# Two transformer blocks on one core: order of the fetches, of the modulation's dots and of the rotary angles at the beginning

## What is computed

```python
mod = jax.nn.silu(c) @ w_ada[l] + b_ada[l]            # w_ada: 1024 x 3072
shift, scale, gate = jnp.split(mod, 3, axis=-1)
h = rmsnorm(x, g_pre[l]) * (1.0 + scale[:, None, :]) + shift[:, None, :]
proj = h @ w_in[l]
...
ang = pos.astype(jnp.float32)[..., None] * inv        # rotary, two bases
cos = jnp.cos(ang); sin = jnp.sin(ang)
...
x = x + gate[:, None, :] * rmsnorm(mixed @ w_out[l], g_post[l])
```

## Time and profile before

| | |
|---|---|
| median of three runs | 1502.81 us |
| lowest, highest | 1500.81, 1503.0 us |
| span of the profiled execution | 1500.5 us |
| what lies around the span, against the median | 2.3 us |
| TensorE busy | 1452.3 us, 97% |
| VectorE, ScalarE, GpSimd busy | 828.7, 683.7, 201.9 us |
| mean granted clock of TensorE | 0.992 |
| chain that ended last | TensorE 84%, VectorE 9%, ScalarE 3% |

### The profile page before, as it was taken

The page is one execution under the profiler, slowest core; times in us unless marked ns, Lnnn a source line. Parts: engine busy times, 40 slices in busy tenths (PEclk is TensorE's granted clock), DMA queues, the critical chain, the costliest instruction groups (busy, mean ns, idle before and its releaser), DMA issues.

```text
span 1500.5 us, 22048 instructions
## 1 busy us (share of the span) xinstructions
PE 1452.3 (97%) x8524; PEld 1226.9 (82%) x8524; DVE 828.7 (55%) x1455; ACT 683.7 (46%) x1302; POOL 201.9 (13%) x319
## 2 busy tenths in 40 slices
PE   7999999899999999999999999989999999999997
PEld 4887876678988888888998777769988888888996
DVE  6678646776645444432275577574754444422474
ACT  4565536676542222221363556676532232321563
POOL 0000000443310000000130222451300000000221
PEclk9999999999999999999999999999999999999999
DMA  9542440004033333333404211503133333332321
GB/s 365 197 167 85 124 157 10 1 2 169 2 99 98 98 98 98 94 95 94 152 3 167 71 57 43 169 16 99 33 109 98 94 92 96 103 105 92 120 85 56
DMA packets 42148, 146.71 MB, mean 98 GB/s; under 512 B 4673, under 2 KB 7121, under 8 KB 41682
## 3 DMA queue, kind: packets, MB, share of 16 engines
q1 hardware_dynamic: 37986, 128.99, 27.2%
q0 software_dynamic: 3072, 15.71, 2.8%
q10 hardware_dynamic: 1008, 0.89, 0.2%
HBM read 141.39 MB, written 4.19 MB: 97 GB/s over the span
## 4 chain that ended last, share of the span: by engine, by line
PE 84%; DVE 9%; ACT 3%; issue 2%; DMA 1%; POOL 0%; DVEq 0%; SPq 0%; ACTq 0%; POOLq 0%
PE B L285 22%; PE B L287 22%; PE B L286 22%; PE CROW_P L285 3%; PE CROW_P L287 3%; PE CROW_P L286 3%; PE B L1789 2%; PE B L2025 1%; DVE AL L1381 1%; DVE WADA L1143 1%; PE CROW_P L1868 1%; ACT T L622 1%; PE CROW_P L1768 1%; ACT AH L622 1%; DVE WL L1110 1%
## 5 line engine op out<-in xcount | busy, mean ns | idle before, releaser
L285 PE MATMUL B<-UH,WH 128*128 128x512 f32 (+1 forms) x1008 | 374.7, 372 | 4.6 <-DVE WL L1110 3.7
L287 PE MATMUL B<-UH,WL 128*128 128x512 f32 (+1 forms) x1008 | 372.3, 369 | 0.0
L286 PE MATMUL B<-UL,WH 128*128 128x512 f32 (+1 forms) x1008 | 372.3, 369 | 0.0
L622 ACT ACTIVATE WH<-RAW 128x1024 fp32r<-128x1024 f32 x174 | 182.6, 1052 | 120.0 <-DMA RAW<-in_stream 111.6
L285 PEld LDWEIGHTS B<-UH,WH 128*128 128x128 f32 x1008 | 190.4, 189 | 38.0 <-issue 5.0
L286 PEld LDWEIGHTS B<-UL,WH 128*128 128x128 f32 x1008 | 190.3, 189 | 32.0
L287 PEld LDWEIGHTS B<-UH,WL 128*128 128x128 f32 x1008 | 190.2, 189 | 32.0
L1110 DVE TENSOR_TENSOR WL<-RAW,WH 128x1024 fp32r<-128x1024 f32 x94 | 116.0, 1240 | 143.8 <-ACT WH L622 143.7
L1462 DVE TENSOR_TENSOR WL<-RAW,WH 128x1024 fp32r<-128x1024 f32 x80 | 98.0, 1226 | 76.7 <-ACT WH L622 73.9
L622 ACT ACTIVATE T<-B 128x256 f32<-128x256 f32 (+5 forms) x186 | 86.5, 465 | 109.9 <-PE B L287 63.3
L622 ACT ACTIVATE T<-T 128x512 f32<-128x512 f32 (+3 forms) x131 | 68.7, 525 | 130.8 <-DVE T L1466 119.2
(11 more groups left out here) (419 smaller groups left out, 3146.2 us busy)
## 6 DMA issues: line engine op xcount, KB each, us to landing
RAW<-in_stream SPq DMA_DIRECT2D x202, 512.0 KB, 3.7
WADA<-in_w_ada SPq DMA_DIRECT2D x8, 1024.0 KB, 16.7
RAW<-in_stream SPq DMA_DIRECT2D x16, 384.0 KB, 3.5
WADA<-in_w_ada SPq DMA_DIRECT2D x2, 2048.0 KB, 11.5
W<-in_w POOLq DMA_DIRECT2D x2, 2048.0 KB, 12.1
X<-in_x SPq DMA_DIRECT2D x2, 1024.0 KB, 11.0
DECAY<-in_decay POOLq DMA_DIRECT2D x1, 2048.0 KB, 9.6
X<-in_x POOLq DMA_DIRECT2D x2, 1024.0 KB, 8.2
```

The costliest lines, as they stand in the source:

```text
L285: nc.tensor.matmul(out, lh, rh, start=start, stop=False, **kw)
L286: nc.tensor.matmul(out, lh, rl, start=False, stop=False, **kw)
L287: return nc.tensor.matmul(out, ll, rh, start=False, stop=stop, **kw)
L622: return nc.scalar.activation(out, in_, func, **kw)
```

## The change

- SyncE's queue fetches x right after c, and pair 0 behind it.
- TensorE warms up with 8 matmuls before the silu row and with 16 behind it, instead of 24 before it.
- SQ has eight tiles, so squares no longer wait for the statistics.
- VectorE does modulation(0) and modulation(1) (`AHEAD = 2`) one after the other; the angles have left its stream.
- GpSimd computes both angles, one after the other, as soon as the positions are there. It has no fused multiply-add here, so each of the three reduction steps is a multiply into T[11] and an add.
- WADA shrinks to 16 rows. The gate's tiles go into rows 8 to 15, once the dots that read these are done, and are fetched ahead of weight tiles 6 and 8.
- The gate's dots run at chunks 6 and 7 (two each) and 8 to 11 (one each). The sines of the second base move from d = 14 to d = 6, `finish_tables(1)` from d = 15 to d = 7.
- DECAY's fetch waits for all 24 dots instead of the scaling of x.

```diff
-        WADA = hb("WADA", 0, [P, ADA, DM])
+        WADA = hb("WADA", 0, [P, 2 * KT, DM])
-        SQ = at("SQ", OFF_U + 16 * KB, [P, 4, SEQ])
+        SQ = at("SQ", OFF_U + 16 * KB, [P, KT, SEQ])
...
             def load_gates(n):
                 m, many = ADA_GATES[n]
-                sp.dma_start(WADA[:, m:m + many, :],
+                sp.wait_ge(E["ada_dot"].sem, 2 * KT - 8 * (1 - n))
+                sp.dma_start(WADA[:, KT + m - 2 * KT:KT + m - 2 * KT + many, :],
...
             sp.dma_start(CROW[0:1, :], a["c"]).then_inc(c_here, 16)
-            load_pair(0)
             for k in range(2):
                 sp.dma_start(X[:, 4 * k:4 * k + 4, :],
...
+            load_pair(0)
...
-                if d in (10, 11):
-                    load_gates(d - 10)
+                if d in (6, 8):
+                    load_gates((d - 6) // 2)
...
-            wait(pool, E["u_t"], KT)
+            def reduced(r, q):
+
+                chain.done(nc.gpsimd.tensor_scalar(q, r, 1.0 / TWO_PI, ROUND, ALU.mult, ALU.add))
+                chain.done(nc.gpsimd.tensor_scalar(q, q, ROUND, None, ALU.subtract))
+                for part in TWO_PI_PARTS:
+                    chain.done(nc.gpsimd.tensor_scalar(T[11][:, :], q, -part, None, ALU.mult))
+                    chain.done(nc.gpsimd.tensor_tensor(r, r, T[11][:, :], ALU.add))
+                E["angle"].mark(nc.gpsimd.tensor_scalar(r, r, PI, -PI, ALU.min, ALU.max))
+
+            pool.wait_ge(pos_here, 16 * 2)
+            chain.done(nc.gpsimd.tensor_copy(T[10][:, :], POSI[:, :]))
+            for n, (r, q) in enumerate(((T[8], T[7]), (T[3], T[2]))):
+                chain.done(nc.gpsimd.tensor_scalar(r[:, :], T[10][:, :], COLS[:, n:n + 1], None, ALU.mult))
+                reduced(r[:, :], q[:, :])
+            wait(pool, E["ada_dot"], ADA)
             fetch(DECAY[:, :, :], a["decay"], decay_here)
...
-                wait(act, E["x_stats"], k - 1 if k >= 4 else 0)
-                return E["x_sq"].mark(f(SQ[:, k % 4, :], src, ACT.Square))
+                return E["x_sq"].mark(f(SQ[:, k, :], src, ACT.Square))
...
-                if d == 14:
+                if d == 6:
                     wait(act, E["angle"], 2)
...
-            modulation(0)
-            dve.wait_ge(pos_here, 16 * 2)
-            chain.done(v.tensor_copy(T[10][:, :], POSI[:, :]))
-            chain.done(ts(T[8][:, :], T[10][:, :], COLS[:, 0:1], None, ALU.mult))
-            chain.done(ts(T[3][:, :], T[10][:, :], COLS[:, 1:2], None, ALU.mult))
-            reduced(T[8][:, :], T[7][:, :])
-            modulation(1)
+            for k in range(AHEAD):
+                modulation(k)
             wait(dve, E["x_rstd"], 2)
...
-                if d == 13:
-                    reduced(T[3][:, :], T[2][:, :])
-                if 12 <= d < 16:
-                    gate_modulation(2 * d - 8, 2 * d - 6)
-                if d == 15:
+                if d in (6, 7):
+                    gate_modulation(2 * d + 4, 2 * d + 6)
+                if 8 <= d < 12:
+                    gate_modulation(d + 12, d + 13)
+                if d == 7:
                     finish_tables(1)
...
             wait(pe, E["converted"], 1)
-            keep_clock(24, UH[:, KT - 1, :], B[4])
+            keep_clock(8, UH[:, KT - 1, :], B[4])
...
+            keep_clock(16, UH[:, KT - 1, :], B[4])
             for k in range(KT):
                 stats(k, B[5])
```

More of the change, by code:

```diff
@@ L59 @@
 FIRST = 6
+AHEAD = 2
 FIRST_STEPS = ([(0, 0), (1, 0), (0, 1), (1, 1)] + [(k, 2) for k in range(2)] + [(2, d) for d in range(3)]
@@ L472, in _ @@
         def _(pool):
+            chain = Chain(pool, "pool_chain")
             def fetch(dst, src, s):
@@ L1131, in _ @@
             E["converted"].mark(v.memset(UH[:, KT - 1, :].bitcast(F32), 0.0))
[L1133 to L1139, removed]
             def dots(m):
-                E["ada_dot"].mark(stt(WADA[:, m, :], WADA[:, m, :], 1.0, (CROW_P if m < 2 * KT else CROW)[:, :], ALU.mult, ALU.mult,
+                row = m if m < 2 * KT else m - KT
+                E["ada_dot"].mark(stt(WADA[:, row, :], WADA[:, row, :], 1.0, (CROW_P if m < 2 * KT else CROW)[:, :], ALU.mult, ALU.mult,
                                       accum_out=DOTS[:, m:m + 1]))
@@ L1191, in _ @@
             for k in range(2, KT):
-                modulation(k)
+                if k >= AHEAD:
+                    modulation(k)
                 u_scaled(k)
@@ L1638, in stats @@
                 wait(pe, E["x_sq"], k + 1)
-                E["x_stats"].mark(mat(bank[:, :], ONES, SQ[:, k % 4, :], start=(k == 0), stop=(k == KT - 1)))
+                E["x_stats"].mark(mat(bank[:, :], ONES, SQ[:, k, :], start=(k == 0), stop=(k == KT - 1)))
             def y_stats(t):
```

## The result

The changed kernel takes 1506.42 us (median of 12 runs, 1504.02 to 1506.8), the kernel before 1502.85 (12 runs beside it, 1500.81 to 1507.24). The ratio is 1.0019, with an interval of 1.0012 to 1.0027: slower by 2.9 us by the ratio and by 3.6 by the medians, small, though the whole interval lies above 1. Another set of 10 runs, later, gave 1504.44 and 1.0015 (1.0004 to 1.0026). The forecast was 1502.9; the medians lie 3.5 us (0.23%) and 1.5 us (0.10%) above it. The profiled execution after has a span of 1504.8 us, where that of before has 1500.5: 4.3 more.

What follows compares the result with a forecast made beforehand. TensorE, busy 97% of the span, was taken as the bound, so only its gaps could close. 1502.8 + 3.0 (later dense run) - 2.9 (gate dots) = 1502.9 us, range 1498.0 to 1506.8.

Steps and rivals of the forecast that it cites:

- The norm comes earlier: Beginning: x lands at 11.4 us, norm's factor comes at 19.2 to 19.5 instead of 22.42, VectorE ready at 19.8.
- Rival 4: Silu row: clock falls, statistics run at half speed, factor at 22; about +0.7, 1503.6 us; chance 0.5 including the main case.
- forecast if the clock were down, 21 to 22: Norm at the beginning: with TensorE's clock down, the factor would arrive at 21 to 22 us.
- What arrives if GpSimd cost nothing: Start of TensorE's dense run: the earlier norm, limited by u_high(1) and the fifth weight tile's landing, gains 1.6 us.
- What the angles cost on GpSimd: Beginning: GpSimd instructions hold VectorE's two-SBUF-input ones, 0.61 us on average, +4.6; dense run 3.0 us later net.
- GpSimd's own time: Beginning: 21 angle instructions from 10.5 us, one-input records 0.77 long, 23 us with waits, done at about 33.
- GpSimd at work beyond 37: Sign at the beginning: GpSimd's angle work lasting past 37 us would point to holds for whole records.
- rival 2: Beginning: GpSimd holds VectorE for whole records, 0.92 on average; 6.8 us plus 1.7 of low clock; 1506.8 us; chance 0.21.
- Gate dots at chunks 6 to 11: Middle: gate loads hidden, the 4.3 us gap near 130 goes, a 1.4 us wait appears; minus 2.9 us net.
- The wait at chunk 12: Chunk 12's first matmul waits for the bank freed by the fourth rotation's multiply: plus 1.4 us.
- Rival 3: Chunk 12: the wait lets the clock fall, as the longer one at 130 did; 1504.3 us; chance 0.1.
- The sum: Whole kernel: 1502.8 + 3.0 - 2.9 = 1502.9 us; what the middle gains is spent at the beginning.

Runs made afterwards that it cites:

- experiment 1: Changed kernel with GpSimd's angle work left out, the angle tiles set to zero: 1500.32 us, 0.998 of the kernel before.
- experiment 3: Changed kernel with all 24 warm-up matmuls ahead of the silu row again: 1503.54 us, 1.0004 of the kernel before.
- experiment 8: Changed kernel run again unaltered, on another occasion; its profiled execution is the "second profile": 1504.44 us, 1.0015 of the kernel before.
- experiment 5: Changed kernel with finish_tables(1) at d = 12 instead of d = 7: 1503.41 us, 1.0002 of the kernel before.
- experiment 2: Changed kernel with a second operation (add 0.0) given to GpSimd's ten one-operation tensor_scalars: 1504.77 us, 1.0008 of the kernel before.
- experiment 7: Changed kernel with GpSimd's angle work replaced by memsets, which only write: one time, 1497.87 us.
- experiment 4: Kernel before with only the gate's part of the change, angles and tables left on VectorE: 1498.97 us, 0.9971 of the kernel before.
- experiment 6: Changed kernel with 24 warm-ups first, all angles on VectorE, second-base sines at d = 13, second tables at d = 14: 1497.78 us, 0.9965 of before.

## Why the prediction came out as it did

**The norm comes earlier: right in some executions, wrong in others.** I had x at 11.4, full clock, the factor at 19.2 to 19.5, and VectorE ready at 19.8. The second half of x is squared from 11.55. Where the clock was up ahead of the row (experiments 1, 3 and 8) x is scaled at 19.5 to 20.1. But in the profile after and in experiment 5 the row took 3.78, some of the 16 warm-ups were slow too (6.3 and 5.7 for all, not 3.95), and the statistics began at 15.2 to 15.4. In experiments 2 and 7 the row was fast (1.98), but then the clock fell while the warm-ups ran (granted 0.50 over 9 to 11 us): they took 5.5, and the statistics began at 12.8 to 13.0. In the six profiles with 8 warm-ups ahead of the row x is thus scaled twice near 19.8, twice near 21.3, twice near 23.7. With 24 ahead of it, as before and in experiments 3, 4 and 6, the row took 1.98 each time. (The statistics behind it took 7.13 in experiments 3 and 6, and 8.83 before and in experiment 4, where TensorE stood idle for 0.8 to 1.0 us ahead of them.) Rival 4 had this clock in mind and put too little on it: it let the statistics run at half speed and added 0.7 us. In fact they run at full speed, but late, and the dense run moves by 3.1. The "forecast if the clock were down, 21 to 22" for the factor was 23.5.

**What arrives if GpSimd cost nothing: right.** Forecast 40.9 to 41.1; experiments 1 and 7 have 41.37 and 41.45. That the factor's first microsecond doesn't arrive is right too: 41.37 comes from x scaled at 20.07, 41.45 from 21.18. The wait for u_high(1) is 0.76 and not 1.2.

**What the angles cost on GpSimd: right mechanism, too large.** Forecast 4.6 net; with the early factor 44.73 - 41.37 = **3.4**. The hold of one instruction was near: forecast 0.48 for one input and 0.95 for two. At 35.74 u_low is stretched by 0.35 beside a one-input instruction, at 41.35 by 1.0 beside a two-input one. What failed is how often the two meet. Ahead of the scaling, four small steps were to cost 1.1, and in the second profile none of them is longer than its plain 0.16. (They can be held: one takes 1.16 in experiment 5, at 17.06, where VectorE had time to spare.) Of the next six instructions each was to wait, for 3.7 in all; they wait 2.8 (in the first profile 1.6, since GpSimd's instruction at 25.21 came second and waited itself while the low half went free). Behind them, where I had 1.0, it is 2.2, because GpSimd worked on until 43. Forecast gross 5.8, found 5.0. The 1.6 between 5.0 and 3.4 are the 1.0 of waits that only experiment 1 has, and the 0.6 by which it scales x later (20.07 against 19.48).

**GpSimd's own time: wrong.** I took 0.77 us for a one-input record from the earlier trace rows, and had the work end at 33; it ended at 43.6. The row I used is a tensor_scalar with two operations, and ten of the 21 have one, which takes 1.50. So the instruction at 40.22 still holds VectorE, for 1.0. By my own list of signs, "GpSimd at work beyond 37" would have meant rival 2. It did not: a 1.50 us record doesn't hold for its length. The scaling at 32.84 takes its plain 0.75 while the record from 31.57 runs to 33.07. The record at 34.83 first waits for the low half to end at 35.8, then holds u_low for 0.35, and runs on for 1.1 us, until 37.18, beside u_low and the dot behind it. That is also why experiment 2 gained nothing in stretch.

**Rival 2** gave 1506.8, and the first median is 1506.42. The agreement is by chance: it needed 6.8 us of holds behind an early factor and a low clock at the dense start. The holds are 3.4 net behind an early factor and 4.0 in the first profile, and the granted clock there is 1.00 from 44.5 to 47.8. The Trainium skill's rule (SBUF — State Buffer, section Who interferes with whom) that the pair is kept for the whole instruction is not borne out here for GpSimd's one-operation form, by the rows at 31.57 and 34.83; for the form with two inputs it is close, with 1.0 of a plain 1.27 us.

**Gate dots at chunks 6 to 11: right.** The wait at chunk 12 was to be 1.4 and is 1.28, ended by the rotation's multiply (T, L1227), as forecast; it costs 1.5 (experiment 5). The gap that went was worth 4.5 (forecast 4.3, experiment 4). Together 2.9 to 3.0, forecast 2.9. Rival 3 didn't happen: the clock stayed up through the wait.

**The sum.** Forecast +3.0 - 2.9 = +0.1. In the second profile it is +2.05 - 2.9 = -0.9, in the first +5.2 - 2.9 = +2.3, and there 1.5 more by the clock that fell near 208 and 0.5 behind it. The base of the sum was also off for a single execution: in every run listed with its span the time is 1.7 to 1.8 us above it, so the profiled execution before, with 1500.5, took some 1502.2 (an estimate) and not 1502.8, which is the median. The step that failed is thus the first: I took one value for the factor, 19.2 to 19.5, where x was scaled near 19.8, 21.3 or 23.7 from one execution to the next. The dense run lay at 47.87 in one profile of this kernel and at 44.73 in the other, and 45.7 was forecast. How often each case comes isn't known, since only profiled executions show it, and there are two of this kernel, one of them the fastest of its set. How much of the 1.5 to 3.5 us between forecast and medians is this, and how much the later falls of the clock, stays open. Experiment 3, which takes this chance away, lies 0.6 us from the forecast (1503.54).

## What to carry to other kernels

Work moved from VectorE to GpSimd is not off VectorE if it reads SBUF: look at what VectorE does at that time, and add up its two-SBUF-input instructions, for each of them can be held (here for up to 1.1 us). The angles were better placed where VectorE was idle for other reasons (experiment 6, 5.1 us faster than before). And when matmuls that warm the clock are cut in two, look at several executions: behind 24 of them the silu row took 1.98 us in all four profiles, behind 8 it took 2.0 to 2.1 in four and 3.78 in two.

## What the runs showed of the hardware that I had not expected

- A GpSimd tensor_scalar of 128x512 with one operation takes 1.50 us, with multiply and add 0.62 (L489 and L486 after). The second operation makes it shorter: L489 falls to 0.62 in experiment 2, and the one with a column operand from 1.56 to 0.69. With subtract and add it is longer, 1.94.
- The long form doesn't hold VectorE longer: about 0.35 us, as the rows at 34.83 and 35.74 show. Where in its record it reads can't be told from the profile.
- A GpSimd instruction that is held by VectorE carries the wait inside its record (2.36 at 40.22, where 1.27 is plain), so a long record is no sign of long work.
- Whether TensorE is at full speed at 5.4 us, behind the same 8 matmuls, differs from one execution of the same program to the next: 3.78 and 2.01 us for the same four matmuls (experiment 8). The granted-clock column reads 1.00 in both, so it doesn't show the first rise.
